# A streaming-encoder layer on one core: exponentials and inverse roots move from ScalarE to GpSimd

## The reference

```python
h = rmsnorm(x, g_mix); proj = h @ w_in            # q k v g | B C h
o = rms_scale(retention(rotary(q), rotary(k), v)) * silu(g)
c = gb * short_conv(gc * hc)
x = x + concat([o, c]) @ w_out
# PEER, per token, on xb = rmsnorm(x, g_ffn):
s1, s2 = q[:, :, 0] . keys1, q[:, :, 1] . keys2   # 8 heads, 128 keys each
# top 16 of each, top 16 of the 256 sums -> top_s and 16 expert numbers eidx
gate = softmax(top_s)
act = gelu(einsum('td,thkd->thk', xb, u_tab[eidx]))
x = x + einsum('thk,thkd->td', gate * act, v_tab[eidx])
y = rmsnorm(x, norm_final_g)
```

## Time and profile before

| | |
|---|---|
| median of 3 runs | 3035.3 us (3033.67 to 3039.89) |
| profiled execution, its own time | 3035.47 us |
| its span in the profile | 3033.6 us |
| first gather issued | 119.27 us |
| last matmul of the last slot starts | 3023.38 us |
| gathers | 1056, 1107.36 of the 1226.64 MB moved |
| granted PE clock, mean | 0.846 |

### The profile page before, as it was taken

The page is one execution under the profiler, slowest core; times in us unless marked ns, Lnnn a source line. Parts: engine busy times, 40 slices in busy tenths (PEclk is TensorE's granted clock), DMA queues, the critical chain, the costliest instruction groups (busy, mean ns, idle before and its releaser), DMA issues.

```text
span 3033.6 us, 36636 instructions
## 1 busy us (share of the span) xinstructions
PE 2303.3 (76%) x12800; PEld 1880.0 (62%) x12800; DVE 2067.1 (68%) x5112; ACT 2044.8 (67%) x3704; POOL 1228.0 (40%) x1060
## 2 busy tenths in 40 slices
PE   9976887787668887877777877888777766667666
PEld 7765776665557766656566665665556555555555
DVE  2466887566688775666888744566588899955454
ACT  1277666668677566776677666667767777676666
POOL 0133333334333333444443344433344445456653
PEclk9987989998889889987887998989888886666666
DMA  7599999999999999999999999999999999999998
GB/s 301 190 416 397 413 408 414 419 420 413 420 421 409 420 417 415 420 404 420 420 416 406 404 422 419 419 419 396 405 420 420 418 418 409 415 418 419 422 420 333
DMA packets 180568, 1226.64 MB, mean 404 GB/s; under 512 B 20736, under 2 KB 21952, under 8 KB 40736
## 3 DMA queue, kind: packets, MB, share of 16 engines
q0 software_dynamic: 152064, 1107.36, 88.6%
q1 hardware_dynamic: 28032, 116.88, 9.6%
q10 hardware_dynamic: 288, 0.07, 0.0%
HBM read 1219.37 MB, written 4.86 MB: 404 GB/s over the span
## 4 chain that ended last, share of the span: by engine, by line
DMA 35%; DVE 24%; PE 22%; ACT 13%; issue 5%; POOL 1%; DVEq 0%; POOLq 0%; ACTq 0%
DMA ring<-in_uv,idx 35%; DVE ring L1459 12%; PE expert_sum L1116 8%; ACT ring L873 5%; PE mm L914 4%; PE x_ps L976 3%; ACT weights L869 2%; PE mm L1038 2%; PE mm L923 2%; ACT L860 1%; DVE pairs_left L1306 1%; ACT dots L860 1%; DVE pairs_left L1394 1%; DVE top_i L1315 1%; DVE pick_f L1400 1%
## 5 line engine op out<-in xcount | busy, mean ns | idle before, releaser
L661 POOL DMA_INDIRECT ring<-in_uv,idx x1056 | 1227.7, 1163 | 1781.8 <-PE expert_sum L1116 1574.7
L1116 PE MATMUL expert_sum<-ident_sb,ring 128*128 128x128 f32 x8448 | 1367.1, 317 | 581.3 <-ACT ring L873 579.8
L1459 DVE CUSTOM_DVE_ANT_0 ring<-ring,xn 128x1024 f32<-128x1024 f32 x1056 | 1286.7, 1223 | 737.8 <-DMA ring<-in_uv,idx 730.2
L1116 PEld LDWEIGHTS expert_sum<-ident_sb,ring 128*128 128x128 f32 x8448 | 1150.5, 165 | 838.6 <-ACT ring L873 767.9
L873 ACT ACTIVATE ring<-ring,weights 128x1024 f32<-128x1024 f32 x1056 | 1213.2, 1149 | 34.3
L860 ACT ACTIVATE dots<-dots 128x1 f32<-128x1 f32 x1056 | 211.5, 200 | 771.6 <-DVE dots L1459 768.2
L869 ACT ACTIVATE weights<-dots,gate 128x1 f32<-128x1 f32 x1056 | 311.1, 295 | 38.2
L914 PE MATMUL mm<-stream,xn_in 128*128 128x256 f32 (+1 forms) x912 | 258.4, 421 | 71.9 <-ACT qkvg L708 56.3
L1038 PE MATMUL mm<-turn,stream 128*128 128x256 f32 (+2 forms) x1024 | 278.4, 401 | 2.8 <-DVE xn_in L1155 2.8
L914 PEld LDWEIGHTS mm<-stream,xn_in 128*128 128x128 f32 (+1 forms) x912 | 166.9, 199 | 113.7 <-ACT qkvg L708 66.0
L923 PE MATMUL mm<-xn_in,stream 128*128 128x256 f32 (+1 forms) x640 | 183.7, 426 | 34.8 <-ACT conv_tmp L699 22.6
(11 more groups left out here) (233 smaller groups left out, 1517.4 us busy)
## 6 DMA issues: line engine op xcount, KB each, us to landing
stream<-in_wq SPq DMA_DIRECT2D x36, 1024.0 KB, 12.0
stream<-in_w_ret SPq DMA_DIRECT2D x26, 1024.0 KB, 9.4
stream<-in_w_conv SPq DMA_DIRECT2D x24, 1024.0 KB, 11.9
ring<-in_uv,idx POOLq DMA_INDIRECT x1056, 12.3
ring<-in_w_ret SPq DMA_DIRECT2D x7, 1024.0 KB, 12.4
x<-in_x SPq DMA_DIRECT2D x8, 512.0 KB, 8.7
w_out_sb<-in_w_out SPq DMA_DIRECT2D x1, 4096.0 KB, 28.9
out_y<-xn SPq DMA_DIRECT2D x8, 512.0 KB, 11.9
```

Of the source, the lines that this page charges most:

```text
L661: pool.indirect_dma_start(ring[:, g % RING, :], None, uv, bass.IndirectOffsetOnAxis(ap=rows, axis=0)).then_inc(landed[g % RING], 16)
L1116: ins = pe.matmul(expert_sum[:, c * P:(c + 1) * P], ring[:, g % RING, D + c * P:D + (c + 1) * P], ident_sb[:, :], is_transpose=True, start ...
L1459: dve.tensor_tensor_reduce(u, u, xn[:, t % 3, :], 1.0, 0.0, ALU.mult, ALU.add, dots[:, g % RING:g % RING + 1]).then_inc(dotted, 1)
```

## The change

ACT keeps Square, Copy, Identity, Tanh, Gelu and one exp, that of tile 0's first head. The other 28 exponentials run on POOL, as e to the power of the score (`tensor_tensor`, op pow, with the constant `euler` broadcast). The 36 roots and reciprocals become a pair on POOL, an addition of 1e-6 and a power of -0.5; the mean is taken by scaling the input of Square by D ** -0.5 (on DVE by 1/P). Silu is g * 0.5 * (1 + tanh(g/2)): tanh on ACT into `qT`, the product with 1 + tanh in a new DVE instruction, the 0.5 in the one that follows retention. POOL gets generators too: before it issues gather g it does what is due at slot g - 8, whose buffer is free by then. ACT's Square of the input norm moves one slot ahead, DVE's norm before PEER two slots back (t > 0), the softmax sums one slot back.

```diff
+            pool.memset(minus_half[:, :], -0.5).then_inc(pool_op, 1)
+            pool.memset(euler[:, :], math.e).then_inc(pool_op, 1)
+            done = [2]
+
+            def root(dst, mean, plus=EPS):
+                n, w = dst.shape[0], dst.shape[1]
+                pool.tensor_scalar(mean, mean, plus, None, ALU.add).then_inc(pool_op, 1)
+                done[0] += 1
+                pool.wait_ge(pool_op, done[0])
+                return pool.tensor_tensor(dst, mean, minus_half[0:n, 0:w], ALU.pow)
+
+            def root_of_x(t):
+                n, r = rows_of(t), RANK[t]
+                yield x_turn_at(t) - 3
+                pool.wait_ge(x_squared, r + 1)
+                root(stat[0:n, 9:10], stat[0:n, 8:9]).then_inc(x_root, 1)
+
+            def root_of_retention(t):
+                n, r = rows_of(t), RANK[t]
+                yield mix_at(t) + 14
+                pool.wait_ge(ret_squared, r + 1)
+                root(stat[0:n, 0:H], stat[0:n, 0:H]).then_inc(ret_root, 1)
+
+            def root_of_x1(t):
+                n, r = rows_of(t), RANK[t]
+                yield out_at(t) + 10
+                pool.wait_ge(x1_squared, r + 1)
+                if r == 0:
+                    pool.wait_ge(first_squared, 2)
+                root(stat[0:n, 5:6], stat[0:n, 4:5], stat[:, 7:8] if r == 0 else EPS).then_inc(x1_root, 1)
+
+            def exponentials():
+
+                for t, first, last in GATES[1:]:
+                    n = rows_of(t)
+                    yield choose_at(last, t) + 6
+                    pool.wait_ge(exp_in, pick(last, t) + 1)
+                    g = gate[0:n, t % 4, first * TOPK:(last + 1) * TOPK]
+                    pool.tensor_tensor(g, euler[0:n, :].broadcast_to([n, (last - first + 1) * TOPK]), g,
+                                       ALU.pow).then_inc(exp_done, 1)
+
+            def root_of_sum(t):
+                n = rows_of(t)
+                yield end_of(t) + 3
+                pool.wait_ge(sum_squared, t + 1)
+                root(stat[0:n, 7:8], stat[0:n, 6:7]).then_inc(sum_root, 1)
+
...
+            programs = started(*[root_of_sum(t) for t in range(TILES + 1)],
+                               *[stage(t) for t in RANK for stage in (root_of_x, root_of_retention, root_of_x1)],
+                               exponentials())
+            for slot in range(FIRST, 0):
+                advance(programs, slot)
             for g in range(TOTAL):
+                if g > RING:
+                    advance(programs, g - RING - 1)
...
+            for slot in range(TOTAL - RING - 1, LAST + 1):
+                advance(programs, slot)
...
-            act.wait_ge(eps_set, 1)
-            act.activation(stat[:, 8:9], eps_sb[:, :], ACT.Sqrt).then_inc(root_table, 1)
 
             def norm(t):
                 n, r = rows_of(t), RANK[t]
-                yield x_turn_at(t) - 3
+                yield x_turn_at(t) - 4
                 x_loaded(act, t)
                 wait(act, x1_ready, GROUPS[group_of(t)][0])
                 if t == SAMPLE:
                     y_stored(act, 3)
-                if r == 0:
-                    act.wait_ge(root_table, 1)
-                else:
-                    act.wait_ge(x_scaled, 2 * r)
-                act.activation(vg_of(t)[0:n, :], x_of(t)[0:n, :], ACT.Square,
+                wait(act, x_scaled, 2 * r)
+                act.activation(vg_of(t)[0:n, :], x_of(t)[0:n, :], ACT.Square, scale=ROOT_D,
                                accum_out=stat[0:n, 8:9]).then_inc(x_squared, 1)
-                act.wait_ge(x_squared, 2 * r + 1)
-                act.activation(stat[0:n, 8:9], stat[0:n, 8:9], ACT.Sqrt, bias=eps_sb[0:n, :],
-                               scale=1.0 / D).then_inc(x_squared, 1)
 
...
-                g = vg_of(t)[0:n, RET:]
-                act.activation(g, g, ACT.Silu).then_inc(silu_done, 1)
+                if scores_before(at):
+                    act.wait_ge(first_keyed, 2)
+                    wait(act, keyed, scores_before(at) - 1)
+                act.activation(qT[0:n, :], vg_of(t)[0:n, RET:], ACT.Tanh, scale=0.5).then_inc(tanh_done, 1)
...
-                yield at + 16
-                act.wait_ge(ret_squared, r + 1)
-                act.activation(stat[0:n, 0:H], stat[0:n, 0:H], ACT.Sqrt, bias=eps_sb[0:n, :],
-                               scale=1.0 / P).then_inc(ret_rooted, 1)
...
-            def exponentials():
-                for t, first, last in GATES:
-                    n = rows_of(t)
-                    yield choose_at(last, t) + 6
-                    act.wait_ge(exp_in, pick(last, t) + 1)
-                    g = gate[0:n, t % 4, first * TOPK:(last + 1) * TOPK]
-                    act.activation(g, g, ACT.Exp).then_inc(exp_done, 1)
+            def first_exponential():
+                yield choose_at(0, 0) + 6
+                act.wait_ge(exp_in, 1)
+                g = gate[:, 0, 0:TOPK]
+                act.activation(g, g, ACT.Exp).then_inc(first_exp_done, 1)
 
...
-                if t == SAMPLE:
-                    act.activation(stat[:, 8:9], eps_sb[:, :], ACT.Sqrt).then_inc(last_table, 1)
...
-                act.wait_ge(sum_squared, 2 * t + 1)
-                act.activation(stat[0:n, 6:7], stat[0:n, 6:7], ACT.Sqrt, bias=eps_sb[0:n, :],
-                               scale=1.0 / D).then_inc(sum_squared, 1)
...
+                yield at + 4
+                dve.wait_ge(tanh_done, r + 1)
+                g = vg_of(t)[0:n, RET:]
+                dve.scalar_tensor_tensor(g, qT[0:n, :], 1.0, g, ALU.add, ALU.mult).then_inc(silu_done, 1)
...
-                op(dve.tensor_tensor(sq, o, o, ALU.mult))
+                op(dve.scalar_tensor_tensor(sq, o, 1.0 / P, o, ALU.mult, ALU.mult))
...
-                dve.wait_ge(ret_rooted, r + 1)
-                op(dve.reciprocal(stat[0:n, 0:H], stat[0:n, 0:H]))
-                settle()
+                dve.wait_ge(ret_root, r + 1)
                 op(dve.tensor_tensor(o, o, bc(stat[0:n, 0:H], 2, P), ALU.mult))
                 settle()
                 dve.wait_ge(silu_done, r + 1)
-                dve.tensor_tensor(o, o, vg_of(t)[0:n, RET:].rearrange("p (h c) -> p h c", h=H),
-                                  ALU.mult).then_inc(gated, 1)
+                dve.scalar_tensor_tensor(o, o, 0.5, g.rearrange("p (h c) -> p h c", h=H),
+                                         ALU.mult, ALU.mult).then_inc(gated, 1)
 
...
-                    dve.wait_ge(x1_squared, 2)
-                    op(dve.reciprocal(stat[:, 5:6], stat[:, 4:5]))
-                    settle()
+                    dve.wait_ge(x1_root, 1)
...
-                yield at + 11
-                dve.wait_ge(x1_squared, 2 * r + 2)
-                op(dve.reciprocal(stat[0:n, 5:6], stat[0:n, 4:5]))
-                settle()
+                yield at + 13
+                dve.wait_ge(x1_root, r + 1)
...
-                    yield choose_at(last, t) + 8
-                    dve.wait_ge(exp_done, b + 1)
+                    yield choose_at(last, t) + (9 if b else 8)
+                    if b:
+                        dve.wait_ge(exp_done, b)
...
```

More of the change, by code:

```diff
@@ L1 @@
+import math
 from contextlib import ExitStack
@@ L36 @@
 EPS = 1e-6
+ROOT_D = D ** -0.5
 LOWEST = -3.0e38
@@ L333, in layer_kernel @@
         eps_sb = sb("eps_sb", [P, 1])
+        minus_half = sb("minus_half", [P, H])
+        euler = sb("euler", [P, 1])
         g_mix_sb = sb("g_mix_sb", [P, KC])
@@ L738, in out @@
                     act.wait_ge(x1_half, 1)
-                    act.activation(xn_of(t)[:, 0:half], x1_of(t)[:, 0:half], ACT.Square,
+                    act.activation(xn_of(t)[:, 0:half], x1_of(t)[:, 0:half], ACT.Square, scale=ROOT_D,
                                    accum_out=stat[:, 6:7]).then_inc(first_squared, 1)
+                    act.wait_ge(eps_set, 1)
                     act.wait_ge(first_squared, 1)
-                    act.activation(stat[:, 7:8], stat[:, 6:7], ACT.Identity, bias=eps_sb[:, :],
-                                   scale=1.0 / D).then_inc(first_squared, 1)
+                    act.activation(stat[:, 7:8], stat[:, 6:7], ACT.Identity, bias=eps_sb[:, :]).then_inc(first_squared, 1)
                     act.wait_ge(x1_ready, 1)
-                    act.activation(xn_of(t)[:, half:], x1_of(t)[:, half:], ACT.Square,
+                    act.activation(xn_of(t)[:, half:], x1_of(t)[:, half:], ACT.Square, scale=ROOT_D,
                                    accum_out=stat[:, 4:5]).then_inc(x1_squared, 1)
-                    act.wait_ge(x1_squared, 1)
-                    act.wait_ge(first_squared, 2)
-                    act.activation(stat[:, 4:5], stat[:, 4:5], ACT.Sqrt, bias=stat[:, 7:8],
-                                   scale=1.0 / D).then_inc(x1_squared, 1)
                     return
@@ L754, in out @@
                     y_stored(act, t - 3)
-                act.activation(xn_of(t)[0:n, :], x1_of(t)[0:n, :], ACT.Square,
+                act.activation(xn_of(t)[0:n, :], x1_of(t)[0:n, :], ACT.Square, scale=ROOT_D,
```

(14 more changed lines are left out.)

29 lines of the change are left out of this document (11 added, 18 removed).

## The result

The changed kernel takes 3123.85 us (median of 5 runs, 3119.43 to 3125.63) against 3035.74 us (5 runs) on the same chip: a ratio of 1.0284, with a 95% interval of 1.0273 to 1.0295. It is 2.8% slower; 3032.4 us were forecast. The profiled execution took 3119.43 us, its span is 3117.6 us.

The account below looks back on a forecast made before the run. DMA bytes were taken to bound the kernel between first and last gathers, dependence chains before and after: 3035.5 - 4.7 (table loads) - 0.2 + 0.6 + 0.7 (pairs) + 0.5 (POOL's code) = 3032.4 us; 8-in-10 range 3024 to 3058.

Parts of the forecast that it names:

- What bounds the kernel: From soon after the first gathers until the last, DMA bytes set the time; start and end are chains of dependences.
- The powers of e: 28 exponentials on POOL: taken at 0.05 us a column, hidden by the DMA queue; 0 (0 to +5.3) us.
- The limit of 7.5 us: Longest power on POOL that costs nothing: the queue bears 6.5 us and 1.0 us of POOL's idling is free.
- rival 1: Wide powers on POOL drain the DMA queue: at 0.15 us a column 30.6 us slower, 3063 us; chance 0.19.
- Behind POOL's wait stand only gathers: At the 32 pairs between gathers: DVE waits for the root slots later, late only if the pair exceeds 5 us.
- The pairs between gathers: 32 root pairs on POOL each delay the next gather by about 1.2 us, against 6.5 us of queue: 0.
- The exposed pairs: Tile 0's norm before PEER, +0.6 (0 to +2.0) us, and the last norm, +0.7 (0 to +2.1) us; nothing covers them.
- Tile 0's retention pair: Pair has 2.0 us of cover under DVE's convolution work and the reciprocal's 0.17 us goes: -0.2 us.
- First arithmetic on POOL: At the program's start, loading code for POOL's first arithmetic may delay tile 0's input norm: +0.5 us.
- the 7 to 8.5 us that I named as its sign: DVE's first tensor_scalar starting at 7 to 8.5 us would confirm the code load's term.
- Table loads: 138 ACT table loads removed; seven DMA dips that follow loads close by share: -4.7 us, between nothing and 8.9 us gain.
- rival 3: ACT's slack is worth more: all eight dips close by bytes and pairs cost 0.5 us; 3024.6 us, chance 0.20.

Follow-up runs that it names:

- idle powers: Changed kernel with exponentials back on ACT (3041.8 us), plus the same 28 powers on POOL on a scratch tile nobody reads: 3086.6 us, ratio 1.0164.
- early norms: Changed kernel with exponentials back on ACT (3041.8 us), Square and POOL root of input norms of tiles 5, 6, 7 four slots earlier: 3034.6 us.
- sums later: Changed kernel with DVE's softmax sums of the wide batches up to twelve slots later: 3101.5 us, ratio 1.0209.
- powers in pieces: Changed kernel with one power of 16 columns for each head on POOL, 71 in place of 28: 3052.0 us, ratio 1.0045.
- exp by tanh: Changed kernel with early norms, last root and exponentials on ACT, exp as (1 + t) / (1 - t), t = tanh(x/2): 3026.1 us, ratio 0.9960.
- products in place of powers: Changed kernel with a multiplication for the power in POOL's 28 instructions, leaving the softmax without its exponential: 3041.9 us, ratio 1.0013.

## Why the prediction was wrong, by its own steps

- **What bounds the kernel.** Right in the main: the last stretch moves 421 GB/s as before, and 71 of the 84 us between the profiled executions lie in stretches in which the DMA engines had nothing to do.
- **The powers of e, 0 (0 to +5.3).** The step that failed. I took 0.05 us a column, half of a range whose upper end, 0.10 us, was no bound at all: a memset of one column says nothing of a power. It is 0.17 us, and the term is +82 us. The limit of 7.5 us held in the sum: by it 10.8 and 21.8 us cost 44 us, and the idle powers cost 44.7. That is rival 1, which I gave 0.19; at its 0.15 us a column it had 30.6 us, at 0.17 it has 44. That the sum is met within 1 us is in part luck, as the powers one by one show.
- **"Behind POOL's wait stand only gathers".** True of POOL and not enough: behind DVE's wait in `gates()` stand the dot products of gathers that have landed. That gave the other 37 us (by subtraction; DVE's sums done later took 22.3 us away), which neither the forecast nor rival 1 had.
- **The pairs between gathers, 0.** Wrong by 7.2 us (early norms). I asked how long the pair takes (0.9 to 1.3 us with one column, 2.0 with four, near the 1.2 that I gave it) and what stands behind it. What stands ahead of it made it late: a gather that waits for PE.
- **The exposed pairs.** Right: 1.08 us from accumulator to use at 104 us for 0.56 (+0.5, forecast +0.6), 1.01 for 0.54 at the end (+0.5, forecast +0.7). Tile 0's retention pair lay under the convolution.
- **The end.** 4.1 us for POOL's closing drain, not in any term.
- **First arithmetic on POOL, +0.5.** The addition starts 0.10 us after ACT's accumulator is read, and DVE's scaling at 6.66 us where it was 6.24: +0.4 by the pair alone, no wait for code, and not the 7 to 8.5 us that I named as its sign. (PE's transposition starts at 9.72 us where it was 9.20, later than the bound that I named, but its input was there at 7.54.) The Trainium skill's (GPSIMD Engine Reference, Instruction dispatch) about 6 us for a first call don't show here: they would have put the root at 8.2 us, and it is there at 6.62. Whether some shorter load of code lies under the 4.88 us in which POOL waits for ACT, the rows can't tell. The first gather comes at 120.13 us, 0.9 us later than before, but in "sums later" and "powers in pieces", which start in the same way, at 118.73 and 118.81 us, so the start's terms are within its scatter.
- **Table loads, -4.7 (0 to -8.9).** Open. With exp by tanh 137 of 140 are gone, and the kernel is 11 us under the one before (0.40%, 8 to 16 us), more than the whole range if the loads did it all; but no run takes loads away and nothing else, and the 56 fewer loads of "products in place of powers" brought nothing. The DMA engines idle no less with exp by tanh than before (14 and 13 us), but move 417.8 in place of 416.7 GB/s between their idle stretches, which makes 7 us. Why is open. (PE "busy without a gap", which I held against rival 3, is true of seven of the eight stretches: at 1310 us it is busy 2.33 of 2.50 us.)

## What to carry to other kernels

Before arithmetic goes to the engine that issues the gathers, get its price in a run by itself: on GpSimd a power of 64 columns took 10.78 us here, twenty times the product of the same size. The longest single instruction counts, not the sum: compare it with the depth of the queue that it must not drain. Of every wait that a move creates ask three things: what stands behind it, what stands ahead of the instruction that it waits for, and what stands behind the engine that waits.

## What was not expected of the hardware

- GpSimd's closing drain takes 8.3 us after its last arithmetic and held the end of the program up by 4.1 us; behind the last gather alone it takes 16.1 us, hidden.
- A product on GpSimd takes 0.35 to 0.57 us for 16 to 64 columns, a power 3.09 to 10.78 us.
- Powers of 64 columns took 10.89 us with DVE busy in 82% of their time, 10.78 with DVE busy in 19% of it: the two engines hardly disturb each other.
